# Value rows of a PEER layer consumed in pairs instead of fours

## The chip, the cores and the metric

One core of a Trainium2 chip runs the whole kernel. The metric is the device time of one execution in microseconds, the median of several runs. The trace numbers come from one profiled execution.

## What is computed

One decoder layer over 1024 positions of width 1024: a token mixer, cross-attention into 256 memory tokens, and a PEER layer, which is the part that the change touches. For each token and each of 8 heads, PEER picks 16 of 16384 single-neuron experts; `u` is the first table and `v` the second:

```python
def per_block(inp):
    xb, eb, gb = inp
    act = jnp.einsum('bthkd,btd->bthk', u[eb], xb).astype(jnp.float32)
    w = (gb * jax.nn.gelu(act, approximate=False)).astype(v.dtype)
    return jnp.einsum('bthk,bthkd->btd', w, v[eb])
```

So each token needs 128 rows of `u` (a dot product with each), and a weighted sum of the same 128 rows of `v`. A layer norm follows.

## The kernel before

The first two stages (the mixer, up to about 1000 us) are not touched. The third, `attend_and_retrieve`, handles tiles of 128 tokens, one token a partition. The first 6 tiles (GATHERED) fetch their expert rows by indirect DMA. The last 2 (DENSE) go through all 16384 experts by dense matrix products instead, in two halves of 64 blocks, woven into the same program.

**Slots.** All engines walk through the same 768 slots (6 tiles x 128 picks), each in its own program order, and meet only at semaphores. In slot g:

- POOL issues the gather of row g of the first table (line 1734, one row of 1024 floats a partition, 512 KB) into a ring of 8 places, then the gather of row g - 20 of the second table (line 1750) into another ring of 8 places. LAG is 20: the weight of a row is known only after its head's 16 dot products.
- DVE takes the dot product of row g with the token (line 2318), and pieces of the next tile's front work (top-16 search, norms).
- ACT spreads the weight of row g - 20 into a 128 x 32 matrix (`spread`, line 2078; `comb` holds four 32-row identities on top of each other), and after each head's 16 dots computes the gelu of 16 weights (line 2062).
- PE multiplies the rows of the second table into `acc` (`combine`, line 1783), runs a piece of the next tile's front (lines 1790 to 1852: transposes, attention scores and values, query and key products), and, from slot 381 on, about one tick a slot of the dense part: `choose` (line 1889, spreads the gates of the dense tokens over the experts of a half), then `dense_u` (line 1901) and `dense_v` (line 1918) for each block in turn.

**The combine.** The tokens of a tile are ordered so that a gathered row belongs to partitions by groups of 32. One matmul takes a spread (128 x 32) as weights and 512 columns of a row as the moving operand and writes the 32 partitions of `acc` that belong to place c = row mod 4. So a quad of rows (SIDE = 4) fills the four groups of 32 array columns side by side; with two halves of 512 columns it is 8 matmuls, each of which appears in the trace as two records. Everything is float32 and accumulates over the 32 quads of a tile; `start` is set on the first quad, `stop` on the last.

**Waits around it.** Each DMA adds 16 to a semaphore. Rows of the second table land on two semaphores (`v_landed`, V_QUADS = 2), quads in turn. PE runs a quad in the slot of its fourth row: it waits for the spreads (`diag_ready`), at the start of a tile for `acc` to have been read (`acc_copied`), and for all four rows; its last matmul adds 1 to `v_used`. POOL, before it gathers row g into a place, and ACT, before it overwrites a spread, wait until `v_used` shows that the quad of row g - 8 is done. With 8 places, the wait changes its value at each fourth row. The last 16 rows (FINAL) have places of their own and land on four semaphores, one for four rows. DVE's layer norm of a finished tile (`norm3_a`, line 2355) waits for `v_used` too and then frees `acc`.

The first half of the slots is filled with front work (each tile's front takes 45 slots). SP issues the dense tables' blocks (512 KB each of `u` and `v`) into rings of three.

## Time and profile before

| | us |
|---|---|
| median of 3 runs | 3616.82 |
| lowest and highest | 3611.86, 3619.35 |
| the profiled execution | 3633.32 (span 3631.3) |

| engine | busy us | share of the span |
|---|---|---|
| PE (matmuls) | 2950.5 | 81% |
| DVE | 2293.9 | 63% |
| POOL | 1848.1 | 51% |
| ACT | 1089.5 | 30% |

The mean granted clock of TensorE is 0.878 of its full rate. 1090.87 MB are moved, 805.40 of them by the indirect gathers. Busy time of PE is modelled from pipelined matmuls, so a share near 100% still leaves room in other kernels. The gathers begin at about 1060 us; from then on all engines have work, and which of them ends the waits has to be read stretch by stretch.

### The profile page before, as it was taken

Reading aid. Unit: us, or ns where it says so; the run is one execution under the profiler, and the core shown is the slowest. Engines: PE = TensorE matmul, PEld = TensorE weight load, DVE = VectorE, ACT = ScalarE, POOL = GpSimd, SP = SyncE. Lnnn points to the kernel's source line nnn. Section 1 sums busy time; section 2 is a strip of 40 time slices with the busy share of each in tenths; the row PEclk is TensorE's granted clock in tenths of the full one; section 3 lists DMA queues with packets and bytes.
Section 4 is the critical chain, followed back from the end, with each engine's and each line's share of the span. In section 5 each row is a group of like instructions: output and inputs, shape, how many; then the busy total and the mean of one; then the engine's idle time right before and its main releaser. Section 6 shows DMA issues by size and latency. Waiting matters only on the chain.

```text
span 3631.3 us, 40464 instructions
## 1 busy us (share of the span) xinstructions
PE 2950.5 (81%) x14096; PEld 1973.7 (54%) x14096; DVE 2293.9 (63%) x4963; ACT 1089.5 (30%) x2864; POOL 1848.1 (51%) x1672
## 2 busy tenths in 40 slices
PE   8999989999995666567756536799999967999994
PEld 6878876665562332323422203477776645777771
DVE  3440047887067677878878768776666667666665
ACT  3320035553123223324323212222222312332222
POOL 3332212221026666666665666666666656666655
PEclk9999999999998877778776766699999867999996
DMA  4322254332459998999999999999999988999998
GB/s 147 117 87 93 93 210 139 95 107 88 162 226 367 351 363 321 352 369 353 364 364 336 391 347 354 362 381 409 409 409 409 402 336 329 409 409 409 409 409 328
DMA packets 313149, 1090.87 MB, mean 300 GB/s; under 512 B 33265, under 2 KB 56433, under 8 KB 309633
## 3 DMA queue, kind: packets, MB, share of 16 engines
q0 software_dynamic: 221184, 805.40, 58.1%
q1 hardware_dynamic: 91776, 283.09, 20.5%
q8 instruction: 103, 1.69, 0.2%
q14 instruction: 86, 0.70, 0.1%
HBM read 1052.12 MB, written 36.24 MB: 300 GB/s over the span
## 4 chain that ended last, share of the span: by engine, by line
PE 23%; DVE 13%; DMA 11%; POOL 9%; issue 7%; another core or an unknown queue 7%; ACT 3%; POOLq 0%; DVEq 0%; ACTq 0%
DMA arena<-in_v_dram,idx_v 9%; PE small L1901 7%; PE wide L1918 6%; PE acc L1783 5%; POOL arena L1750 5%; DVE arena L2318 3%; POOL far_rows L1734 2%; POOL arena L1734 2%; DVE far_rows L2318 2%; PE small L1840 2%; DMA arena<-in_u_dram,idx 2%; DVE arena L2593 1%; ACT gelu_v L2062 1%; DVE arena L2591 1%
## 5 line engine op out<-in xcount | busy, mean ns | idle before, releaser
L1750 POOL DMA_INDIRECT arena<-in_v_dram,idx_v x752 | 801.9, 1066 | 686.5 <-PE acc L1783 357.4
L1783 PE MATMUL acc<-arena 128*32 128x512 f32 x3008 | 497.2, 778 | 423.9 <-DMA arena<-in_v_dram,idx_v 217.3
L1734 POOL DMA_INDIRECT arena<-in_u_dram,idx x480 | 498.3, 1038 | 344.3 <-DVE idx L2554 190.5
L1783 PEld LDWEIGHTS acc<-arena 128*32 128x32 f32 x3008 | 100.0, 129 | 693.4 <-issue 529.4
L1901 PE MATMUL small<-pwq 128*128 128x256 f32 x2048 | 467.0, 381 | 2.0 <-ACT memory_tables L2179 1.7
L1901 PEld LDWEIGHTS small<-pwq 128*128 128x128 f32 x2048 | 386.6, 190 | 84.1 <-issue 28.8
L2318 DVE CUSTOM_DVE_ANT_0 arena<-arena,wide 128x1024 f32<-128x1024 f32 x294 | 355.1, 1216 | 73.6 <-DMA arena<-in_u_dram,idx 44.1
L1734 POOL DMA_INDIRECT far_rows<-in_u_dram,idx x288 | 302.5, 1050 | 92.3 <-issue 81.7
L2318 DVE CUSTOM_DVE_ANT_0 arena<-arena,h 128x1024 f32<-128x1024 f32 x186 | 226.5, 1224 | 183.2 <-DMA arena<-in_u_dram,idx 180.2
L2318 DVE CUSTOM_DVE_ANT_0 far_rows<-far_rows,wide 128x1024 f32<-128x1024 f32 x176 | 212.8, 1216 | 60.8 <-DMA far_rows<-in_u_dram,idx 42.3
L2189 ACT ACTIVATE arena<-small 128x256 f32<-128x256 f32 x128 | 49.2, 385 | 656.0 <-PE small L1901 484.5
L2078 ACT ACTIVATE arena<-comb,w_v 128x32 f32<-128x32 f32 x768 | 198.9, 311 | 153.0 <-remote 60.5
L433 PE MATMUL group<-w_nat_high,x_parts 128*128 128x512 f32 x768 | 240.6, 395 | 3.8 <-ACT arena L572 3.8
L927 PE MATMUL mix_bank<-memory_tables,mixT 128*128 128x512 f32 x512 | 226.4, 598 | 3.6 <-ACT mixT L1178 3.6
L898 POOL TENSOR_TENSOR arena<-arena 128x512 f32<-128x512 f32 (+1 forms) x48 | 48.1, 1001 | 346.3 <-DVE arena L1288 344.5
L2062 ACT ACTIVATE gelu_v<-act_u 32x4 f32<-32x4 f32 x768 | 159.4, 208 | 206.1 <-DVE act_u L2318 144.7
L1889 PEld LDWEIGHTS small<-arena 128*128 128x128 f32 x1024 | 165.0, 253 | 90.4 <-issue 64.1
L433 PE MATMUL group<-x_parts,arena_rounded 128*128 128x512 f32 x864 | 202.0, 395 | 10.7 <-DVE x_parts L606 10.7
L1889 PE MATMUL small<-arena 128*128 128x64 f32 x1024 | 172.7, 341 | 43.6 <-DVE arena L2595 22.6
L2318 DVE CUSTOM_DVE_ANT_0 far_rows<-far_rows,h 128x1024 f32<-128x1024 f32 x112 | 136.5, 1223 | 97.2 <-DMA far_rows<-in_u_dram,idx 90.0
L433 PEld LDWEIGHTS group<-x_parts,arena_rounded 128*128 128x128 f32 x864 | 163.7, 190 | 49.4 <-issue 10.1
L1918 PE MATMUL wide<-arena_rounded 128*128 128x512 f32 x512 | 181.4, 436 | 0.0
(376 smaller groups left out, 4973.2 us busy)
## 6 DMA issues: line engine op xcount, KB each, us to landing
pwq<-in_uT_dram SPq DMA_DIRECT2D x128, 512.0 KB
pwq<-in_v_dram SPq DMA_DIRECT2D x128, 512.0 KB
arena<-in_w_nat_dram SPq DMA_DIRECT2D x6, 2048.0 KB, 8.6
nat_dram<-stage SPq DMA_DIRECT2D x48, 256.0 KB, 2.1
arena<-in_v_dram,idx_v POOLq DMA_INDIRECT x752
scanT_dram<-stage SPq DMA_DIRECT2D x22, 512.0 KB, 2.9
arena<-in_w_tr_dram SPq DMA_DIRECT2D x18, 512.0 KB, 3.7
arena<-csT_dram SPq DMA_DIRECT2D x8, 1024.0 KB, 4.8
```

Of the source, the lines that this page charges most:

```text
L433: last = pe.matmul(to, stationary(p, k), moving(q, k), start=(k == 0 and n == 0), stop=(k == KC - 1 and n == 2))
L927: last = pe.matmul(place["OUT"][:, c * 512:(c + 1) * 512], mixT[:, k, :], w_out[:, k, c * 512:(c + 1) * 512], start=(k == 0), stop=(k == 2 ...
L1734: pool.indirect_dma_start(out=u_row(g), out_offset=None, in_=peer_u, in_offset=bass.IndirectOffsetOnAxis(ap=idx[:, t % KEPT, n:n + 1], axis=0)
L1750: pool.indirect_dma_start(out=v_row(g), out_offset=None, in_=peer_v, in_offset=bass.IndirectOffsetOnAxis(ap=idx_v[:, t % KEPT, n:n + 1], a ...
L1783: last = pe.matmul(acc[c * QUAD:(c + 1) * QUAD, half * 512:(half + 1) * 512], spread_row(at), v_row(at)[:, half * 512:(half + 1) * 512], s ...
L1840: last = pe.matmul(small[:, q * P:(q + 1) * P], pwq[:, k, q * P:(q + 1) * P], hT[:, k, :], start=(k == 0), stop=(k == KC - 1))
L1889: last = pe.matmul(small[:, at:at + HALF_KEYS], hot2[:, q % 2, j, :], hot1[:, q % 2, j, :], start=True, stop=True)
L1901: last = pe.matmul(small[:, at:at + DT], uT_ring[:, i % STREAM, k, :], dense_hT[:, k, :], start=(k == 0), stop=(k == KC - 1))
L1918: last = pe.matmul(wide[:, at:at + 512], w, v[:, c * 512:(c + 1) * 512], start=(i % HALF_KEYS == 0 and n == 0), stop=(i % HALF_KEYS == HAL ...
L2062: last = act.activation(gelu_v[r * QUAD:(r + 1) * QUAD, h % 2, :].rearrange("p (b c) -> p b c", c=SIDE)[:, :, c], act_u[c * QUAD:(c + 1) * ...
L2078: act.activation(spread_row(g), comb[:, :], ACT.Copy, scale=w_v[:, h % 2, j:j + 1]).then_inc(diag_ready, 1)
L2318: dve.tensor_tensor_reduce(out=row, in0=row, in1=against, scale=1.0, scalar=0.0, op0=ALU.mult, op1=ALU.add, accum_out=act_u[:, (n // TOPK) ...
```

## The change

Rows of the second table are handled in pairs. They land on four semaphores in turn (V_PAIRS = 4) instead of two; PE waits for two rows, multiplies them (4 matmuls) and adds 1 to `v_used`, in each second slot instead of each fourth; POOL and ACT wait for the pair of row g - 8 instead of its quad; the norm waits for twice the count. The column group of a row is still its place mod 4, so a pair uses two of the four groups. The four semaphores of the last 16 rows stay as they are, but their rows are multiplied in pairs too. Ring size, bytes, gathers, spreads and matmuls stay the same in number.

```diff
--- before.py
+++ after.py
@@ -29,7 +29,8 @@
 U_RING = 8
 V_NEAR = 8
 V_RING = 8
-V_QUADS = 2
+V_PAIRS = 4
+PAIR = 2
 KEYS_ROW = 2
 QUAD = 32
 SIDE = 4
@@ -1492,7 +1493,7 @@
         VALUE_TABLE = 14
         FIRST_ALL = VALUE_TABLE + KC
         u_landed = [sem(f"u_landed{i}") for i in range(U_RING)]
-        v_landed = [sem(f"v_landed{i}") for i in range(V_QUADS)]
+        v_landed = [sem(f"v_landed{i}") for i in range(V_PAIRS)]
         final_landed = [sem(f"final_landed{i}") for i in range(FINAL // SIDE)]
         dot_done = sem("dot_done")
         gelu_done = sem("gelu_done")
@@ -1617,7 +1618,7 @@
 
         def v_signal(g):
 
-            return final_landed[final_place(g) // SIDE] if final_place(g) >= 0 else v_landed[g // SIDE % V_QUADS]
+            return final_landed[final_place(g) // SIDE] if final_place(g) >= 0 else v_landed[g // PAIR % V_PAIRS]
 
         def spread_row(g):
 
@@ -1746,7 +1747,7 @@
                     if final_place(g) == 0:
                         pool.wait_ge(vb_used, NKEYS)
                     elif V_RING <= g < SLOTS - FINAL:
-                        pool.wait_ge(v_used, (g - V_RING) // SIDE + 1)
+                        pool.wait_ge(v_used, (g - V_RING) // PAIR + 1)
                     pool.indirect_dma_start(out=v_row(g), out_offset=None, in_=peer_v,
                                             in_offset=bass.IndirectOffsetOnAxis(ap=idx_v[:, t % KEPT, n:n + 1], axis=0)
                                             ).then_inc(v_signal(g), 16)
@@ -1768,21 +1769,21 @@
                 def combine(t, s, n):
 
                     g = PICKS * t + n
-                    if n % SIDE < SIDE - 1:
+                    if n % PAIR < PAIR - 1:
                         return
                     pe.wait_ge(diag_ready, g + 1)
-                    if n == SIDE - 1 and t > 0:
+                    if n == PAIR - 1 and t > 0:
                         pe.wait_ge(acc_copied, t)
                     if final_place(g) >= 0:
                         pe.wait_ge(final_landed[final_place(g) // SIDE], 16 * SIDE)
                     else:
-                        pe.wait_ge(v_landed[g // SIDE % V_QUADS], 16 * SIDE * (g // SIDE // V_QUADS + 1))
+                        pe.wait_ge(v_landed[g // PAIR % V_PAIRS], 16 * PAIR * (g // PAIR // V_PAIRS + 1))
                     for half in range(2):
-                        for c in range(SIDE):
-                            at = g - SIDE + 1 + c
+                        for at in range(g - PAIR + 1, g + 1):
+                            c = at % SIDE
                             last = pe.matmul(acc[c * QUAD:(c + 1) * QUAD, half * 512:(half + 1) * 512],
                                              spread_row(at), v_row(at)[:, half * 512:(half + 1) * 512],
-                                             start=(n == SIDE - 1), stop=(n == PICKS - 1))
+                                             start=(n < SIDE), stop=(n >= PICKS - SIDE))
                     last.then_inc(v_used, 1)
 
                 def to_T(source):
@@ -2074,7 +2075,7 @@
                     if g == 0:
                         act.wait_ge(comb_ready, SIDE)
                     if V_RING <= g < SLOTS - FINAL:
-                        act.wait_ge(v_used, (g - V_RING) // SIDE + 1)
+                        act.wait_ge(v_used, (g - V_RING) // PAIR + 1)
                     act.activation(spread_row(g), comb[:, :], ACT.Copy,
                                    scale=w_v[:, h % 2, j:j + 1]).then_inc(diag_ready, 1)
 
@@ -2644,7 +2645,7 @@
                         elif n == 2 and t > 0:
                             weigh(t - 1, 1 - s, PHEADS - 1)
                         if n == LAG and t > 0:
-                            norm3_a(t, h2[:, 1 - s, :], acc[:, :], v_used, PICKS // SIDE * t)
+                            norm3_a(t, h2[:, 1 - s, :], acc[:, :], v_used, PICKS // PAIR * t)
                         if n == LAG + 4 and t > 0:
                             norm3_b(t, h2[:, 1 - s, :])
                         slot = PICKS * t + n
@@ -2665,7 +2666,7 @@
 
                 def last(t, s):
                     weigh(t - 1, 1 - s, PHEADS - 1)
-                    norm3_a(TILES, h2[:, 1 - s, :], acc[:, :], v_used, PICKS // SIDE * t)
+                    norm3_a(TILES, h2[:, 1 - s, :], acc[:, :], v_used, PICKS // PAIR * t)
                     norm3_b(TILES, h2[:, 1 - s, :])
 
                 tiles(body, last)
```

## Rows read from the trace of the kernel before

**Rows 1.** The page's slices: GB/s moved in each fortieth of the span.
```profile
GB/s 147 117 87 93 93 210 139 95 107 88 162 226 367 351 363 321 352 369 353 364 364 336 391 347 354 362 381 409 409 409 409 402 336 329 409 409 409 409 409 328
```
**Rows 2.** Stretches: length, then busy us (records) of PE, PEld, DVE, ACT, POOL; clock, DMA, GB/s.
```profile
1110.00:2060.00 950.00, 613.40 (x2952) 301.04 (x2951) 732.60 (x2191) 298.00 (x951) 603.18 (x618) 0.78 0.95 355
2060.00:2180.00 120.00, 39.57 (x202) 10.72 (x200) 82.41 (x299) 27.22 (x100) 74.99 (x80) 0.65 0.94 361
2180.00:2380.00 200.00, 136.89 (x750) 90.88 (x754) 167.59 (x249) 49.47 (x160) 131.38 (x135) 0.65 0.96 357
2380.00:2865.00 485.00, 467.08 (x2304) 350.78 (x2297) 305.86 (x524) 141.78 (x384) 302.96 (x252) 0.99 1.02 406
2865.00:3080.00 215.00, 148.33 (x833) 102.11 (x832) 156.17 (x238) 53.23 (x173) 133.54 (x134) 0.70 0.91 342
3080.00:3550.00 470.00, 454.02 (x2239) 342.33 (x2241) 295.53 (x508) 135.85 (x362) 290.10 (x242) 0.99 1.03 409
```
**Rows 3.** The same stretches, line 1783 alone: PE busy (records), PEld busy (records), clock, DMA.
```profile
1110.00:2060.00 950.00, 215.48 (x1248) 41.98 (x1248) 0.78 0.95 355
2060.00:2180.00 120.00, 35.06 (x160) 6.58 (x160) 0.65 0.94 361
2180.00:2380.00 200.00, 53.52 (x264) 10.12 (x268) 0.65 0.96 357
2380.00:2865.00 485.00, 64.43 (x508) 14.44 (x500) 0.99 1.02 406
2865.00:3080.00 215.00, 50.95 (x256) 9.53 (x256) 0.70 0.91 342
3080.00:3550.00 470.00, 60.37 (x492) 14.14 (x496) 0.99 1.03 409
sum 2521.00, PE 510.97 PEld 103.28; mean PE 73.00 PEld 14.75
```
**Rows 4.** Line 1783 from 1110 to 2060: ns of one record, min/median/max.
```profile
L1783 PE MATMUL acc<-arena x1248: 589/617/1063, 1112.2 to 2058.1; 128*32 128x512 f32 x179
```
**Rows 5.** Timeline of PE in a dense stretch: start, us, work, idle before it.
```profile
2574.68 1.92 PE L1783 MATMUL acc<-arena 128*32 128x512 f32 x16 [1.09 <-DMA arena<-in_v_dram,idx_v]
2576.53 3.72 PE L1901 MATMUL small<-pwq 128*128 128x256 f32 x16
```
**Rows 6.** Timeline of PE among front work of a gathering stretch.
```profile
1805.76 1.92 PE L1783 MATMUL acc<-arena 128*32 128x512 f32 x16
1807.61 7.13 PE L1808 MATMUL wide<-memory_tables,arena 128*128 128x512 f32 x16
...
1826.36 3.64 PE L1783 MATMUL acc<-arena 128*32 128x512 f32 x16 [9.15 <-DMA arena<-in_v_dram,idx_v]
```
**Rows 7.** Waits from 1110 to 2060: who <- releaser: us in total, times, longest us.
```profile
POOL arena L1750 <- remote: 100.8, 43, 4.1
PE acc L1783 <- DMA arena<-in_v_dram,idx_v: 78.9, 17, 10.5
POOL arena L1750 <- PE acc L1783: 72.5, 17, 12.0
PE acc L1783 <- ACT arena L2078: 63.5, 10, 16.1
```
**Rows 8.** Waits in the dense stretch from 2380 to 2865.
```profile
POOL arena L1750 <- PE acc L1783: 112.4, 29, 10.0
...
PE acc L1783 <- DMA arena<-in_v_dram,idx_v: 16.7, 14, 4.1
```
**Rows 9.** Timeline of POOL in the gathering stretch.
```profile
1807.75 0.94 POOL L1750 DMA_INDIRECT arena<-in_v_dram,idx_v  x1 [0.30 <-issue]
1809.00 0.94 POOL L1734 DMA_INDIRECT arena<-in_u_dram,idx  x1 [0.31 <-issue]
1812.43 0.94 POOL L1750 DMA_INDIRECT arena<-in_v_dram,idx_v  x1 [2.49 <-remote]
```
**Rows 10.** The end of PE's work in its timeline.
```profile
3615.32 6.16 PE L1783 MATMUL acc<-memory_tables,arena 128*32 128x512 f32 x40 [1.08 <-issue]
```

## The prediction

> **What bounds the kernel now.** The table of stretches is read first [rows 1, 2]. From 1110 to 3631 us the rows of the two tables are gathered, and this part has two regimes. In the two stretches with the dense products of the last tokens (2380 to 2865 and 3080 to 3550), the DMA engines move 406 and 409 GB/s, the flat maximum of the slices [rows 1], and at the same time PE is busy for 467.1 of 485 and 454.0 of 470 us. Two resources are full at once. In the others neither is: from 1110 to 2060 PE is busy for 613.4 of 950 us at a mean granted clock of 0.78, DVE for 732.6, and 355 GB/s are moved. The second reading is PE's line 1783 alone [rows 3], the third what four rows cost PE [rows 4 to 6], the fourth who waits in each regime [rows 7 to 9].
>
> **How many combines.** A quad leaves 16 matmul records. The dense stretches hold 508 + 492 = 1000 records, 62.5 quads in 955 us, one each 15.28 us. The stretch from 1110 to 2060 holds 1248, 78 quads, one each 12.18 us, a slot (one row of each table) each 3.05 us. The stretches 2180 to 2380 and 2865 to 3080, where PE picks the gates of the dense tokens, hold some 32.
>
> **What a pair costs on PE.** This is the term that decides. A quad's 16 records take 1.92 us though one record takes 592 or 617 ns [rows 4, 5]: 16 one after another would be 9.5 us or more. A full-width record of the same 512 columns comes each 7.13 / 16 = 0.446 us [rows 6]. So 1.92 us is four rounds of about 0.43 us plus one tail of about 0.19, four records side by side in each round, one for each group of 32 columns. A group of columns has four records to run (two halves, two records each) whatever its neighbours do. A pair has 8 records, two in each of the same four rounds: 1.92 us as a quad, and twice in four slots. Rivals of this price: 0.96 us, if a combine's time goes by its records and not by its rounds (then the change adds nothing), and 8 x 0.446 = 3.6 us, if nothing ran side by side. I take 1.85 us, the time from a quad's first record to the start of the next work (2574.68 to 2576.53), since the rounds fit the quad's rows with nothing left over. Where the clock is low a quad takes 3.64 us [rows 6]; the mean from 1110 to 2060 is 215.48 / 78 = 2.76 us.
>
> A combine also switches PE between column groups and the full array. The Trainium skill, TensorEngine Tiling (Array Packing), Key Properties, says that a change of the tiling mode drains the engine. No row shows a drain by itself. The 1.85 us holds what the way out of a quad costs, and the sum would be the same with a drain named.
>
> **Part by part.** The four spreads on ACT, the gathers on POOL and the bytes stay the same in number: no cost. The waits on PE grow from one set in four slots to two; they are sequencer work, counted at nothing where the condition holds.
>
> *Dense stretches.* PE's work is 467.08 + 454.02 = 921.1 us. It gets 62.5 more combines x 1.85 = 115.6, so 1036.7 us, more than the 955 us there are. If all its idle time (33.9 us, mostly the wait for landed rows, 16.7 us in the first stretch [rows 8]) vanishes, the stretches grow by 81.7 us; if it all stays, by 115.6. The wait should mostly go, as rows come in more often than PE can take them: **+88**. POOL's stall here (112.4 us on PE's line 1783 in the first stretch [rows 8]) costs nothing today, because the queue behind it is full at 406 GB/s; freeing places earlier buys nothing.
>
> *Gathering stretch 1110 to 2060.* This is where the change can win. POOL issues a gather each 1.24 us [rows 9], so eight (four of each table) take 9.95 us, against 12.18. The difference is its stalls: 100.8 us put down to "remote" and 72.5 to PE [rows 7], 173.3 in all. All of them stand before the first row of a quad, as in [rows 9] (2.49 us): that row needs the release of the quad two back, whose last row was issued five slots earlier. In pairs, the row needs a pair whose last row was issued seven slots earlier: two slots, about 5 us, more room. Most stalls are shorter than that, and would go. But three floors stand below. POOL: 950 - 173.3 = 777 us. DMA: 355 x 950 / 409 = 825 us. PE: 613.4 + 215.5 (the combines again, at their mean of today) = 829 us. PE is the highest, and it can't run full: it waits today for landings (78.9 us) and for ACT's spreads (63.5 us) [rows 7]. Kept whole, these 142 us bring 971 us, 21 more than today; gone, 829, 121 less. As PE falls behind the gathers, landings are there when it comes, but the spreads' chain (DVE's dots, ACT's gelu, DVE's product) is not shortened, and it now holds PE at the second row and not at the fourth. I keep some 76 us, about half: 829 + 76 = 905, **-45**, from +21 to -121.
>
> *Stretches 2180 to 2380 and 2865 to 3080.* PE 136.9 + 148.3 = 285.2, plus 53.5 + 51.0 = 104.5, is 389.7 of 415 us, 94%. Little to win, little to lose: **+5**, from -25 to +40.
>
> *2060 to 2180.* PE has only combines: 39.6 + 35.1 = 75 of 120 us, hidden. Eight gathers take 12 us as before against 9.95 at POOL's own pace, most of it in one long stall: **-5**, from 0 to -18 (10 quads at 2 us, less what DMA holds back).
>
> *Start of a tile.* The first combine of a tile waits until DVE has taken acc over, now two slots earlier. At five tile borders this costs nothing if DVE is in step, up to 2 x 3.05 us each (30 us) if it lags as far; no row shows PE waiting for it: 0, the other end goes into the range.
>
> *The end.* The last 16 rows are still waited for in fours but multiplied in pairs. Behind the last wait 40 records run in 6.16 us with nothing beside them [rows 10]; their rounds nearly double: **+5**, from +2 to +6.
>
> Sum: 88 - 45 + 5 - 5 + 5 = **+48 us**. The profiled execution took 3633.32 us (span 3631.3), 16.5 above the median of the runs; the same difference is carried over: 3633.3 + 48 = 3681 profiled, 3616.8 + 48 = **3665** as median.
>
> **Rivals.**
>
> *The room wins (faster).* The gathering stretch falls to its floor. What would bring it there is the clock: rows with a busier PE show a higher granted clock (0.99 at 96% busy, 0.78 at 65%, 0.65 at 33%) [rows 2]. If twice the combines lift the clock to the higher of its two levels, 2.4 GHz, a quad's 2.76 us becomes 1.92, PE's floor falls to about (613.4 - 215.5) x 0.78 + 2 x 78 x 1.92 = 610 us, and DMA's 825 decides: -125; with -25 and -18 in the other two and +82 and +5 that is -81: 3536. Against it: 0.65 and 0.70 at 68% busy between 2180 and 3080, so the link is loose, and DVE at 733 of 825 us would be 89% full in an order of its own. It decides the sign as soon as the stretch from 1110 to 2060 gives back more than the dense stretches take, that is from some 85 us on. The Trainium skill, TensorE: Matmul & The Clock Gate, in the part on the clock gate, says that the throttled state is the default and activity releases it; by that rule this case is the likelier one, and the rows agree in direction only.
>
> *The pair is cheap (faster).* At 0.96 us a pair, dense stretches +0 and the gathering stretch -121: about 3490.
>
> *It comes out even.* PE keeps a third of its waits in the gathering stretch and the pick stretches gain 10: within 7 us of 3617.
>
> *PE is late everywhere (slower still).* None of its waits shrinks: +116, +21, +40, 0, +6: 3800; with half of that beyond my sum 3735. It decides where the wait for spreads moves two slots up at each head.
>
> *The change does nothing at the ring.* If the stalls called "remote" are no matter of places but of the release itself coming late (PE's quad at 1805.76 is over at 1807.68 [rows 6], POOL goes on at 1812.43 [rows 9]), each pair could bring such a stall, and the gathering stretch gains nothing: +93, 3710. This is inside the slower side.
>
> **How the numbers follow.** A measurement of this kernel can tell about 0.2% (7 us) from no change. Forecast, PE as bound with part of the stalls won back: 0.48. The release rival: 0.12. PE late everywhere: 0.08. Even: 0.06. The room wins: 0.20. Cheap pair: 0.06. So slower 0.68, same 0.06, faster 0.26. The likeliest case's own range is 3625 to 3710; to hold eight in ten the range reaches up to half of the late case and down to near the rival in which the room wins: 3555 to 3745.
>
> **What would show it.** In the profile after: 8 records of line 1783 in 1.9 us in the dense stretches (1.0 would be the cheap pair), so that its busy time goes from 511 us towards 950; dense stretches over 1020 us long, PE at 97% or more there, and GB/s under 380 with POOL's stalls on PE still there; from 1110 on, the part of POOL's idle time before line 1750 halved, with PE over 85% busy. Wrong if the dense stretches keep their 955 us, or if the gathering stretch ends more than 90 us earlier.

## The result, and the profile after

| | before, us | after, us |
|---|---|---|
| median | 3614.34 (4 runs) | 3692.52 (4 runs) |
| lowest and highest | 3608.30, 3619.35 | 3691.01, 3703.22 |
| profiled execution | 3633.32 | 3691.36 |

The ratio is 1.0221, with a 95% interval of 1.0188 to 1.0253: the change makes the kernel slower by 78 us, where 48 were forecast (3665). The median of before is over one run more than the 3616.82 that the forecast started from. The two profiled executions differ by 58 us, because that of before lay 19 us above its own median of 3614.34 and that of after 1 us below its own.

For where the 58 us are, each trace is cut at the same instructions: the first gather of the second table, the first transpose of the dense tokens, the first record of the dense products in each half (line 1901 of before), the first record of `choose` of the second half, and the last record of the dense products (line 1918). "Picking" stands for the two gate-picking stretches. All tables of stretches below are made in this way, in us, from these starts:

| | gathering | picking 1 | dense 1 | picking 2 | dense 2 | tail |
|---|---|---|---|---|---|---|
| before | 1035.1 | 264.0 | 492.2 | 193.0 | 481.0 | 77.7 |
| after | 1040.3 | 256.0 | 532.0 | 178.1 | 524.0 | 71.8 |
| difference | +5.2 | -8.0 | +39.8 | -14.9 | +43.0 | -5.9 |

The differences add up to 59, because after the first gather came 1 us earlier. The dense stretches took 82.8 us more, against the forecast's 88. The gathering stretch, which was to give 45 back, gave nothing, and the gate-picking stretches and the tail gave 29 where next to nothing was expected.

After, in stretches that answer to [rows 2] (length; busy us and records of PE, PEld, DVE, ACT, POOL; clock, DMA share, GB/s):
```profile
1105.00:2058.00 953.00, 703.23 (x2976) 305.61 (x2972) 730.35 (x2199) 300.43 (x958) 611.50 (x625) 0.87 0.96 358
...
2383.00:2915.00 532.00, 527.44 (x2296) 357.67 (x2296) 302.67 (x532) 145.63 (x394) 287.23 (x252) 1.00 0.99 378
2915.00:3093.00 178.00, 146.99 (x754) 83.95 (x752) 138.25 (x211) 43.93 (x154) 114.62 (x120) 0.81 0.95 350
3093.00:3617.00 524.00, 523.46 (x2285) 356.72 (x2286) 296.54 (x522) 141.01 (x382) 285.11 (x250) 1.00 0.99 377
```
In both dense stretches PE is busy for 99% of the time or more (527.4 of 532, 523.5 of 524) and DMA has fallen from 406 and 409 GB/s to 378 and 377: of the two resources that were full, PE alone now sets the time, although the DMA share still reads 0.99. After, the combine's line alone (PE, PEld, clock, DMA share, GB/s), which answers to [rows 3]:
```profile
1105.00:2058.00 953.00, 327.44 (x1248) 62.44 (x1244) 0.87 0.96 358
...
2383.00:2915.00 532.00, 121.51 (x504) 23.93 (x504) 1.00 0.99 378
```
As many records as before take 121.5 us in place of 64.4. After, PE's timeline in a dense stretch (start, us, work), to be held against [rows 5]:
```profile
2506.13 1.91 PE L1784 MATMUL acc<-arena 128*32 128x512 f32 x8
2507.97 3.72 PE L1902 MATMUL small<-pwq 128*128 128x256 f32 x16
...
2514.37 1.91 PE L1784 MATMUL acc<-arena 128*32 128x512 f32 x8
```
Eight records of a pair take as long as a quad's sixteen, and pairs come each 8.24 us, so four slots take 16.48 us in these rows, against a mean of 15.28 before. After, who waits, in the gathering stretch (who <- releaser: us, times, longest), against [rows 7]:
```profile
PE acc L1784 <- ACT arena L2079: 88.4, 27, 12.7
PE acc L1784 <- issue: 83.3, 21, 15.9
...
POOL arena L1751 <- remote: 69.6, 30, 4.3
POOL arena L1751 <- PE acc L1784: 67.9, 37, 8.6
```
and in the first dense stretch, against [rows 8]:
```profile
ACT arena L2190 <- PE small L1902: 284.5, 50, 6.7
POOL arena L1751 <- PE acc L1784: 183.9, 62, 7.0
```
PE's 78.9 us of waiting for landed rows don't appear in the gathering stretch after, those for spreads grew from 63.5 to 88.4, and POOL's two stalls shrank only from 173.3 to 137.5. The wait for rows isn't simply gone: "issue", idle time for which the profile shows no releaser, was at the same line before
```profile
PE acc L1783 <- issue: 52.6, 19, 16.0
```
and is 83.3 us now. In all PE sat idle before its combines for 195.0 us before and 171.7 after.

### The profile page after: what moved, and what is told of

Read it like the earlier page. It is cut to its first block, busy times and chain, and to the rows that moved or that the text cites. A ratio compares the mean times of both kernels' runs of the same rounds, so it can differ in the third digit from the quotient of the medians.

```text
span 3689.4 us, 40656 instructions
## 1 busy us (share of the span) xinstructions
PE 3197.0 (87%) x14096; PEld 1973.7 (53%) x14096; DVE 2272.0 (62%) x4963; ACT 1088.7 (30%) x2864; POOL 1815.2 (49%) x1672
## 4 chain that ended last, share of the span: by engine, by line
PE 39%; DVE 16%; issue 7%; another core or an unknown queue 6%; ACT 3%; POOL 2%; DMA 1%; POOLq 0%; DVEq 0%; ACTq 0%
PE small L1902 12%; PE acc L1784 10%; PE wide L1919 10%; DVE arena L2319 4%; DVE far_rows L2319 3%; PE small L1890 2%; PE wide L1809 1%; PE small L1841 1%; ACT gelu_v L2063 1%; POOL arena L1751 1%; PE wide L1824 1%; DVE arena L2594 1%; DVE idx_v L2552 1%; DVE gates_v L2552 1%
## 5 line engine op out<-in xcount | busy, mean ns | idle before, releaser
L1751 POOL DMA_INDIRECT arena<-in_v_dram,idx_v x752 | 764.4, 1017 | 742.3 <-PE acc L1784 460.3
L1784 PE MATMUL acc<-arena 128*32 128x512 f32 x3008 | 798.1, 675 | 306.0 <-ACT arena L2079 169.4
L1735 POOL DMA_INDIRECT arena<-in_u_dram,idx x480 | 496.4, 1034 | 368.8 <-DVE idx L2555 190.7
L1784 PEld LDWEIGHTS acc<-arena 128*32 128x32 f32 x3008 | 153.7, 117 | 743.5 <-issue 530.2
L2319 DVE CUSTOM_DVE_ANT_0 arena<-arena,wide 128x1024 f32<-128x1024 f32 x294 | 353.7, 1212 | 34.7 <-DMA arena<-in_u_dram,idx 14.3
L2603 DVE TENSOR_TENSOR memory_tables<-memory_tables,arena 128x256 f32<-128x256 f32 x128 | 55.2, 432 | 432.6 <-ACT arena L2190 229.6
L434 PE MATMUL group<-x_parts,arena_rounded 128*128 128x512 f32 x864 | 201.9, 395 | 10.9 <-DVE x_parts L607 10.9
L1890 PEld LDWEIGHTS small<-arena 128*128 128x128 f32 x1024 | 136.8, 212 | 101.4 <-issue 84.0
L1890 PE MATMUL small<-arena 128*128 128x64 f32 x1024 | 147.2, 299 | 33.2 <-issue 28.1
## 6 DMA issues: line engine op xcount, KB each, us to landing
nat_dram<-stage SPq DMA_DIRECT2D x48, 256.0 KB, 2.2
```

The costliest lines, as they stand in the source:

```text
L434: last = pe.matmul(to, stationary(p, k), moving(q, k), start=(k == 0 and n == 0), stop=(k == KC - 1 and n == 2))
L1735: pool.indirect_dma_start(out=u_row(g), out_offset=None, in_=peer_u, in_offset=bass.IndirectOffsetOnAxis(ap=idx[:, t % KEPT, n:n + 1], axis=0)
L1751: pool.indirect_dma_start(out=v_row(g), out_offset=None, in_=peer_v, in_offset=bass.IndirectOffsetOnAxis(ap=idx_v[:, t % KEPT, n:n + 1], a ...
L1784: last = pe.matmul(acc[c * QUAD:(c + 1) * QUAD, half * 512:(half + 1) * 512], spread_row(at), v_row(at)[:, half * 512:(half + 1) * 512], s ...
L1890: last = pe.matmul(small[:, at:at + HALF_KEYS], hot2[:, q % 2, j, :], hot1[:, q % 2, j, :], start=True, stop=True)
L2319: dve.tensor_tensor_reduce(out=row, in0=row, in1=against, scale=1.0, scalar=0.0, op0=ALU.mult, op1=ALU.add, accum_out=act_u[:, (n // TOPK) ...
```

## The experiments

They ran in three sets, each with runs of the kernel before among them. The kernel before had a median of 3448.77 us in the first set, 3631.82 in the second and 3447.88 in the third, so only kernels of one set are compared in time. "Theory" and the letters stand for what each expectation says.

### First set: the price of a pair

The kernel before and the change again, to have both traces in this set:

> The kernel before, profiled a second time. The result is 78 us slower by the medians, but the two profiled executions differ by 58 us only; the first profile of before lay 19 us above its median. Theory: this is one slow profiled execution, and a second profile of before has its span near 3612, the missing 20 us in the gathering stretches (up to the first dense product at 2387 us), where semaphores decide, not in the dense stretches, which a full DMA queue fixes at 492 and 481 us. Rival: profiling itself costs before 16 to 19 us and the second profile repeats 3630.

> The changed kernel again, on one chip with the others. Expected 3690 to 3700 us and 1.019 to 1.025 of before; dense stretches of 532 and 524 us as in its first profile.

Before: 3447.58 us in its one run. After: 3529.82 (3526.40 to 3530.46), a ratio of 1.0233 (1.0217 to 1.0249). The ratio and the dense stretches (532.1 and 524.0 us, table below) are as expected. The times are not, and neither 3612 nor its rival 3630 for the trace of before can be judged, since the gathering and gate-picking stretches are faster here.

`fours_by_two` keeps fours, but orders the quad's matmuls as two pairs one after the other:
```diff
-                    for half in range(2):
-                        for c in range(SIDE):
-                            at = g - SIDE + 1 + c
+                    for first in (0, 2):
+                        for half in range(2):
+                            for c in (first, first + 1):
+                                at = g - SIDE + 1 + c
...
```


> Waits, ring and releases in fours as before; only the order of a quad's 8 matmuls is changed: rows 0 and 1 with both halves, then rows 2 and 3, so that two column groups work side by side and not four. It has PE's price without the granularity of two. Theory (the price is rounds on PE): the 8 matmuls take 7 to 8 rounds of 0.43 us, 3.2 to 3.8 us for 1.9, the two dense stretches grow by 70 to 100 us together, the gathering stretch by 20 to 80, and the whole is at or above the changed kernel: 3690 to 3780. Rival (records count, not rounds; the slower time comes from waiting in pairs): 1.9 us a quad and 3615.

3449.34 us (3444.89 to 3459.10), ratio 1.0006 (0.9997 to 1.0016): no difference. The theory, 3.2 to 3.8 us a quad, is refuted. The rival's numbers came, though not for its reason, since eight records of the change take as long as sixteen. `pairs_crossed` is the change with the second half of each row moved to the two column groups that the pair leaves idle. The accumulator's second half then lies in other partitions, and the norm reads it from there:
```diff
-                            c = at % SIDE
+                            c = (at + 2 * half) % SIDE
...
-                    dve.scalar_tensor_tensor(y3, y3, ALPHA, total, ALU.mult, ALU.add).then_inc(acc_copied, 1)
...
+                        dve.scalar_tensor_tensor(y3[:, 0:HALF_D], y3[:, 0:HALF_D], ALPHA, total[:, 0:HALF_D], ALU.mult, ALU.add)
+                        for to, source in ((slice(0, 64), slice(64, 128)), (slice(64, 128), slice(0, 64))):
+                            last = dve.scalar_tensor_tensor(y3[to, HALF_D:D], y3[to, HALF_D:D], ALPHA,
+                                                            total[source, HALF_D:D], ALU.mult, ALU.add)
...
```


> Waits, ring and releases in pairs as in the changed kernel, but the second half of a row's columns goes to the column group two places on, so that a pair's 4 matmuls fill all four groups: two rounds a pair, four rounds in four slots as before. The norm puts the halves right with two more vector operations at each of the 6 tiles (about 0.6 us each). It has the granularity of two without PE's price. Theory: a pair takes 1.0 to 1.1 us, the dense stretches come back to 960 to 980 us, and what pairs bring by themselves shows in the gathering stretch: its stalls on line 1750 fall from some 160 us to under 100, for 3560 to 3600 in all, faster than before. Rival 1 (granularity brings nothing, the gathering stretch is held by the chain of dots, gelu and spreads): 3610 to 3625. Rival 2 (each combine has a fixed cost that twice as many pay): 3640 or more.

3466.68 us (3465.32 to 3471.95), ratio 1.0058 (1.0044 to 1.0072): slower than before, not faster as its theory had it. A quad in `fours_by_two`, and a pair in `pairs_crossed`, in the dense stretch (PE's timeline of each):
```profile
2408.70 1.94 PE L1784 MATMUL acc<-arena 128*32 128x512 f32 x16 [1.15 <-DMA arena<-in_v_dram,idx_v]
```
```profile
2403.59 1.06 PE L1784 MATMUL acc<-arena 128*32 128x512 f32 x8
```

| first set | gathering | picking 1 | dense 1 | picking 2 | dense 2 | tail |
|---|---|---|---|---|---|---|
| before | 925.9 | 228.1 | 490.5 | 159.0 | 480.9 | 76.8 |
| after | 935.5 | 223.7 | 532.1 | 152.4 | 524.0 | 72.2 |
| `fours_by_two` | 926.2 | 228.4 | 490.2 | 159.0 | 480.7 | 76.9 |
| `pairs_crossed` | 926.0 | 239.0 | 484.9 | 173.3 | 475.5 | 78.1 |

The order in which a quad's matmuls are issued doesn't matter (1.94 us): within a batch the four groups of columns still run side by side. What costs is that a pair offers work to only two of the four groups. With all four in use the same 8 records take 1.06 us, and the 84.7 us that the dense stretches of the change cost here not only vanish but turn into a gain of 11.0. The gathering stretch gained nothing from the pairs (926.0 against 925.9). The Trainium skill, TensorEngine Tiling (Array Packing), Key Properties, states that different tiles can load weights and multiply in parallel; 1.06 and 1.91 us for the same eight records show what it means when only half of them have work.

But `pairs_crossed` loses 10.9 and 14.3 us in the gate-picking stretches. Its stretches (columns as above):
```profile
2014.00:2253.00 239.00, 198.98 (x871) 124.56 (x871) 207.94 (x373) 63.18 (x207) 166.15 (x172) 0.51 1.00 392
...
2738.00:2911.00 173.00, 171.05 (x753) 117.41 (x752) 147.03 (x223) 44.88 (x155) 119.87 (x123) 0.50 1.01 394
```
and those of the kernel before in this set:
```profile
2010.00:2238.00 228.00, 154.68 (x874) 96.92 (x870) 206.76 (x375) 63.10 (x206) 166.08 (x173) 0.66 1.02 400
2729.00:2888.00 159.00, 113.19 (x753) 76.50 (x753) 144.58 (x220) 45.14 (x155) 117.70 (x122) 0.81 1.02 407
```
PE, with half the time per pair, is granted 0.51 and 0.50. In the second of these stretches it is busy for 171 of 173 us: at the lower of its two levels it has become the bound there. In the first it is busy for 199 of 239. This gave a theory for the second and third sets.

### Second set: price without the finer waits, and the clock

`fours_in_two_parts` is the kernel before, with places 0 and 1 of a quad multiplied where the quad was and places 2 and 3 after the slot's other work:
```diff
+                    multiply(g, n, (0, 1))
+
+                def multiply(g, n, places):
                     for half in range(2):
-                        for c in range(SIDE):
+                        for c in places:
...
-                    last.then_inc(v_used, 1)
+                    return last
+
+                def combine_rest(t, s, n):
+                    if n % SIDE == SIDE - 1:
+                        multiply(PICKS * t + n, n, (2, 3)).then_inc(v_used, 1)
...
                             dense(tick)
+                        if n >= LAG or t > 0:
+                            combine_rest(*lagged(t, s, n))
...
```


> The kernel before, its waits, its four-row releases and its two landing semaphores unchanged; only PE's work of a quad is cut in two: places 0 and 1 are multiplied where the quad was, places 2 and 3 after the same slot's front or dense work. So PE pays the price of pairs (two batches that each use two of the four column groups) while nothing is waited for or given back in pairs. Theory A (the price of a pair on PE is the whole loss of the dense stretches): each batch of 8 records takes 1.9 us, the dense stretches are 80 to 86 us longer than before's 971 (490 and 481), the rest within 5 us, a ratio of 1.020 to 1.026, as the change itself has. Theory B (the loss comes from waiting or releasing in pairs): dense stretches within 10 us of before, a ratio of 0.998 to 1.004.

3752.50 us (3749.28 to 3758.76), ratio 1.0342 (1.0309 to 1.0375). Its timeline and its first dense stretch:
```profile
2459.54 1.91 PE L1786 MATMUL acc<-arena 128*32 128x512 f32 x8
...
2464.35 1.91 PE L1786 MATMUL acc<-arena 128*32 128x512 f32 x8
...
2476.04 1.91 PE L1786 MATMUL acc<-arena 128*32 128x512 f32 x8
```
```profile
2422.00:2954.00 532.00, 527.51 (x2304) 357.63 (x2304) 307.91 (x533) 145.63 (x394) 303.51 (x255) 1.00 0.99 379
```
The dense stretches are those of the change to the tenth (532.3 and 524.1 against 532.0 and 524.0), four slots in 16.50 us in these rows, though it waits and releases in fours. So in these stretches the price of the two batches is the whole loss, as theory A had it. The ratio is above A's range all the same: outside of them this kernel takes 1600.8 us, against 1558.0 to 1585.3 of the three others of its set (below), while the change was 24 us shorter there than before in its own set. Its release comes only after the second batch, later than that of before, so how much of the excess is the batch and how much the lateness isn't told apart.

The next two kernels put matmuls with zero weights, which add nothing to the sum, ahead of a batch, outside of the dense stretches. `fours_zeros` does it to the kernel before and `crossed_zeros` to `pairs_crossed` (the lines shown are those of `crossed_zeros`):
```diff
+        def outside(g):
+
+            slot = g + LAG
+            dense = any(tick_slot(h * HALF_TICKS + GROUP_TICKS) <= slot < (tick_slot(HALF_TICKS), DENSE_END)[h] for h in range(2))
+            return slot >= DENSE_AT and not dense
...
+                    if outside(g) and n > SIDE:
+                        pe.wait_ge(zeros_ready, 1)
+                        for half in range(2):
+                            for at in range(g - PAIR + 1, g + 1):
+                                c = (at + 2 * half) % SIDE
+                                pe.matmul(acc[c * QUAD:(c + 1) * QUAD, half * 512:(half + 1) * 512],
+                                          zeros[:, :], v_row(at)[:, half * 512:(half + 1) * 512], start=False, stop=False)
```


> The kernel before, with each quad's 8 matmuls preceded by 8 more whose weights are zero (they add nothing to the sum), outside the dense stretches alone: in the two stretches in which PE picks the gates, the one just before the first, and the tail. It asks what the granted clock does when PE has some 2 us more work in four slots there, while waits and releases stay in fours. Theory A (the changed kernel's shorter gate-picking stretches come from a higher granted clock that its busier PE gets): clock there from 0.66 and 0.81 up to 0.80 and 0.93 or so, the two stretches 4 to 8 us shorter in sum than before's 387, a ratio of 0.996 to 0.999. Theory B (they come from waiting and releasing in pairs): the clock may rise but the stretches don't shorten, or grow by up to 15 us with the added work: 1.000 to 1.005.

3648.97 us (3632.28 to 3652.76), ratio 1.0039 (1.0020 to 1.0059).

> The crossed pairs (the two halves of a pair go to different column groups, so all four run), with 4 more zero-weight matmuls ahead of each pair's 4, outside the dense stretches alone. The crossed pairs were 11 us shorter than before in the dense stretches and 25 us longer in the two gate-picking stretches, where the granted clock was 0.51 and 0.50. Theory A (those 25 us are the clock's, which fell because PE had less to do): the clock there is 0.8 or more, the stretches return to the plain pairs' 376 in sum against 412, dense stays at 960, and the kernel is 15 to 25 us below before, 0.993 to 0.996. Theory B (they come from another cause, such as the norm's read of the crossed accumulator): clock up or not, the stretches stay over 400, 1.004 to 1.008.

3616.79 us (3598.58 to 3626.38), ratio 0.9961 (0.9941 to 0.9982). `mixed` takes pairs only where `outside` holds for the quad (`in_pairs`), and fours elsewhere, with the release counted in pairs throughout:
```diff
+        def used(g):
+
+            return g // PAIR + 1 if in_pairs(g) else 2 * (g // SIDE + 1)
...
-                        pool.wait_ge(v_used, (g - V_RING) // SIDE + 1)
+                        pool.wait_ge(v_used, used(g - V_RING))
...
-                    last.then_inc(v_used, 1)
+                    last.then_inc(v_used, size // PAIR)
```


> Fours in the gathering and in the two dense stretches, plain pairs (waited for, multiplied and given back) only in the two gate-picking stretches and the tail, with four landing semaphores throughout. Theory A (a pair costs in the dense stretches alone, where PE and DMA are both full, and gains 11 us in the gate-picking stretches and 5 in the tail): dense 971, gate-picking 376 in sum against 387, tail 72 against 77, a ratio of 0.995 to 0.998. Theory B (the gain in those stretches only answers the state that the pairs elsewhere leave, such as the rows already waiting): within 0.1% of before or above.

3620.87 us (3614.14 to 3636.16), ratio 0.9984 (0.9965 to 1.0002).

| second set | gathering | picking 1 | dense 1 | picking 2 | dense 2 | tail |
|---|---|---|---|---|---|---|
| `fours_in_two_parts` | 1055.7 | 273.7 | 532.3 | 190.7 | 524.1 | 80.7 |
| `fours_zeros` | 1042.6 | 269.6 | 492.4 | 181.7 | 479.2 | 91.4 |
| `crossed_zeros` | 1019.7 | 275.6 | 484.5 | 187.8 | 473.8 | 84.7 |
| `mixed` | 1032.9 | 269.0 | 487.9 | 178.2 | 481.3 | 77.9 |

This set has no trace of the kernel before. `fours_zeros` and `mixed` do the same work in fours up to the first gate-picking stretch, and they differ by 9.7 us there: a stretch of one execution can't be read closer than some 10 us here. Their second gate-picking stretch, `fours_zeros` first:
```profile
2897.00:3079.00 182.00, 151.88 (x1000) 88.46 (x992) 143.09 (x219) 44.73 (x154) 118.52 (x121) 0.79 0.96 353
```
```profile
2878.00:3056.00 178.00, 141.50 (x752) 80.38 (x752) 142.35 (x218) 44.49 (x155) 116.27 (x121) 0.83 0.98 373
```
The gate-picking stretches of `fours_zeros` are no shorter than those of `mixed`, the clock is no higher, and the tail is 13.5 us longer. Theory A's ratio and its clock for the second stretch (0.93) didn't come, and the whole kernel lost 17 us, most of it in the tail. Without a trace of before in this set it isn't known whether its gate-picking stretches are shorter than before's, so where the clock comes from is left open by it. `crossed_zeros` has the better ratio and the 958 us of dense stretches of A, but its gate-picking stretches (463.4 us in sum) are longer than those of `mixed` (447.2); A's 376 came from a set with faster gathers and can't be held against them. `mixed` lies within its interval of no change. Its dense stretches (969.2) are as A had them, its tail is not: 77.9 us with pairs, where A had 72 and before has 76.3 to 77.7 in all its traces. So pairs in the tail alone don't shorten it, which speaks for B there; for the rest its theories are neither shown nor refuted.

### Third set: the clock on its own

The kernel before, the change, the crossed pairs again, and the crossed pairs with zeros in the gate-picking stretches alone:
```diff
-            return slot >= DENSE_AT and not dense
+            return DENSE_AT <= slot < DENSE_END and not dense
```


> The kernel before, once more, for a trace of it on the same chip as the next three. No theories differ. On the first chip its stretches from the first row of the second table on were 1035, 264, 492, 193, 481 and 78 us (gathering, gate-picking, dense, gate-picking, dense, tail).

> The changed kernel, once more. Theory A (the price of a pair on PE is paid in the dense stretches wherever it runs, the rest depends on the chip): dense stretches together 80 to 86 us over those of the trace of before on this chip, 20 to 30 less in the other four together if gathering runs at 355 GB/s, 0 to 10 less if it runs at 400; ratio 1.020 to 1.026. Theory B (the loss depends on the chip): anything outside that.

> The crossed pairs without zero-weight matmuls. On one chip they were 11 us shorter in the dense stretches and 25 longer in the gate-picking ones, with a granted clock of 0.51 and 0.50. Theory A (the clock falls because PE's work per pair is halved): the clock in the gate-picking stretches is below that of before here (0.50 to 0.60), these stretches are 10 to 30 us longer in sum than with zeros, ratio 1.002 to 1.008. Theory B (the crossed kernel without zeros is as fast as with them, and the zeros only cost): clock 0.65 or more, ratio 0.993 to 0.998. If rows gather at 355 GB/s here, the gathering stretch tells what the pair's price on PE took from it: crossed pairs 10 to 25 us shorter there than the changed kernel (PE's share) or within 5 us (DMA's).

> The crossed pairs with 4 zero-weight matmuls a pair in the gate-picking stretches alone, no longer in the tail, where four-row records with zeros had made it 14 us longer (91 against 78). Theory A (the zeros are worth their price where PE has other work to bring under the higher clock, and cost where only combines are left): the tail 5 to 9 us shorter than the 85 us with zeros, the rest as with them, ratio 0.991 to 0.996. Theory B (the tail's length follows the clock, and without zeros it grows by as much): ratio 0.996 to 0.999.

| third set | median, us | ratio | gathering | picking 1 | dense 1 | picking 2 | dense 2 | tail |
|---|---|---|---|---|---|---|---|---|
| before | 3447.88 | | 923.2 | 228.2 | 490.2 | 156.8 | 483.3 | 76.3 |
| after | 3524.06 | 1.0224 (1.0204 to 1.0245) | 935.3 | 222.5 | 532.0 | 150.0 | 524.0 | 72.2 |
| `crossed_third` | 3465.03 | 1.0050 (1.0035 to 1.0065) | 925.8 | 239.0 | 484.9 | 173.1 | 476.3 | 77.0 |
| `crossed_zeros_choose` | 3443.30 | 0.9990 (0.9981 to 0.9999) | 926.3 | 222.6 | 490.9 | 157.9 | 480.3 | 78.7 |

The trace of before is its one run of 3446.53 us. The change does what theory A of its expectation says: +82.5 us in the dense stretches, 4.5 less in the other four together. For `crossed_third` the clock and the ratio are theory A's; its gate-picking stretches are 31.6 us longer than with zeros, where A had 10 to 30. `crossed_third`, PE's timeline in the second gate-picking stretch, and below it the same of `crossed_zeros_choose`:
```profile
2802.49 1.94 PE L1784 MATMUL acc<-arena 128*32 128x512 f32 x8
2804.35 3.68 PE L1890 MATMUL small<-arena 128*128 128x64 f32 x16
2807.96 1.94 PE L1784 MATMUL acc<-arena 128*32 128x512 f32 x8
```
```profile
2812.25 1.06 PE L1793 MATMUL acc<-arena,zeros 128*32 128x512 f32 x8
2813.13 1.04 PE L1798 MATMUL acc<-arena 128*32 128x512 f32 x8
```
Their rows of the two gate-picking stretches, `crossed_third` first:
```profile
2014.00:2253.00 239.00, 198.94 (x871) 124.23 (x871) 207.80 (x373) 63.15 (x207) 167.25 (x172) 0.51 1.00 392
...
2738.00:2911.00 173.00, 171.30 (x753) 117.70 (x753) 147.06 (x223) 45.02 (x155) 119.95 (x124) 0.50 1.01 395
```
```profile
2013.00:2236.00 223.00, 159.48 (x1107) 86.12 (x1104) 206.52 (x370) 63.29 (x207) 165.41 (x170) 0.80 1.02 405
...
2727.00:2885.00 158.00, 139.02 (x994) 80.76 (x995) 144.19 (x219) 45.31 (x156) 116.89 (x122) 0.87 1.02 405
```
With 29% more records (2101 against 1624), PE is busy for 72 us less: at 0.50 a pair and its share of `choose` follow each other without a gap, 5.47 us in two slots; with zeros the clock is 0.80 and 0.87 and the two stretches are 31.6 us shorter. That is shown, by adding work alone: the crossed kernel's 25 to 27 us in these stretches were the clock's. The Trainium skill, TensorE: Matmul & The Clock Gate, in its Part 1, says that the gate is set by "how busy the PE has been recently"; here more work brought more clock, though the share of busy time in the records was the higher one (171 of 173 us) at the lower level.

Yet the dense stretches, 12 us under before in `crossed_third`, give 10 of these back. The stretches of picking and dense 1 together take 718.4 us before, 723.9 crossed and 713.5 with zeros; those of the second half 640.1, 649.4 and 638.2. With zeros the DMA share is 1.02 or 1.03 and the rate 404 to 409 GB/s in every stretch up to the tail. The reading is that the bytes set the time there, so a cheaper combine has nothing to win: length times GB/s gives 491 x 409 = 200.8 MB in dense 1 with zeros and 485 x 403 = 195.5 in `crossed_third`, whose slow gate-picking stretch had moved most of the difference beforehand. The tail is 78.7 us against 77.0 without zeros anywhere. The 84.7 us it was to be measured against belong to another set, but the tail of before hardly differs between the sets, so this speaks for theory A's tail without settling it. The total (0.9990) is outside theory A's range and at the edge of B's. Of all kernels run, the crossed pairs with zeros are the only ones whose interval lies below the kernel before: 0.9961 in the second set, with zeros in the tail too, and 0.9990 here. No run shows a use of the pair that is worth more than that.

## Why the prediction was right or wrong

**The price of a pair: right.** Four rounds whatever the number of groups, 1.92 us at the full clock; it measured 1.91. Its two rivals (0.96 and 3.6 us) fell in the trace after, and `pairs_crossed` and `fours_by_two` show why it is so. 1.06 us for crossed pairs also bears out the rounds of about 0.43 us and one tail of about 0.19: two rounds and the tail are 1.05.

**The dense stretches: right.** +88 forecast, +82.8, +84.7 and +82.5 in the three traces of after beside one of before, close to the floor of 81.7 at which PE has no idle time left. `fours_in_two_parts`, with the same dense stretches and the waits of before, shows that waiting in pairs has no part in it.

**The gathering stretch: wrong.** -45 was forecast, +5.2, +9.6 and +12.1 measured. The step that failed is the one that makes PE the bound there, 829 us of work plus 76 us of kept waits. Both parts were mis-sized. The clock rose to 0.87 and a pair cost 327.44 / 156 = 2.10 us in place of a quad's 2.76, so PE had work for 703 of 953 us, not for 829. And its idle time before was 950 - 613 = 337 us, of which only the 142 of two waits were counted: by the same sum the kernel before would have taken 613 + 142 = 755 us there. After, 250 us of idle time are left, and PE's work doesn't set the length.

The second step that failed is the room: "two slots, about 5 us, more room", by which most of POOL's stalls would go. The records of line 1750 and of the combines can be matched by their order. Before, 45 of the 78 gathers of a quad's first row start more than 0.6 us after both the modelled end of the quad that they need and the end of POOL's instruction before; after, 42 of 156 at the first row of a pair; in the third set 6 of 83 and 4 of 168. So for most stalls called "remote" (100.8 us before, 69.6 after) the place was free already, and more room could not help. They are in the slower gatherings alone. What they are was not found.

DMA's floor, "355 x 950 / 409 = 825", is not what failed in the sum, as 905 lies above it. In the first and third sets the gathering stretch of before is full (before of the third set):
```profile
1100.00:2010.00 910.00, 604.18 (x3073) 291.48 (x3074) 786.49 (x2387) 319.46 (x1032) 646.15 (x669) 0.82 1.02 403
```
and there no handling of places can win. For the traces of the prediction (355 GB/s at a share of 0.95 [rows 2], 406 at 1.02 in the dense stretch) the share would give an estimate of 950 x 0.95 / 1.02 = 885 us. But the dense stretches of after, where PE is the bound, read 0.99, so a share near 1 doesn't show that the bytes decide. The traces' packets tell more. In the first dense stretch, 166 of 48739 packets of 4 KB took over 200 ns before, and 1785 of 48962 after. In the gathering stretch 3806 of 82249 did before and 3856 of 83012 after, but 659 of 88450 in the third set. By this the slower gathering is like a stretch that the bytes don't bound. What bounds it, neither PE's work nor plainly the bytes, stays open.

**Gate-picking stretches and tail: wrong in size and, for the tail, in sign.** +5 (and a part of the -5) was forecast and -22.9 measured, -11.0 and -12.5 in the other sets; the tail -5.9 instead of +5. The cause is not shown. The first of these stretches lies ahead of both dense ones. In the third set, before and then after, it is
```profile
2010.00:2238.00 228.00, 155.43 (x871) 95.79 (x871) 207.49 (x375) 63.40 (x207) 165.09 (x171) 0.66 1.02 400
```
```profile
2023.00:2246.00 223.00, 169.31 (x873) 85.71 (x872) 206.00 (x368) 63.33 (x207) 166.98 (x172) 0.88 1.03 409
```
The same 91.2 MB (length times GB/s) moved at a higher rate, with a higher granted clock. For the second one and the tail the rows suggest a coupling: a dense stretch that gets longer leaves DMA room, in which rows and blocks land ahead. Of the third set, before and then after, from the first dense stretch to the end:
```profile
2238.00:2728.00 490.00, 468.20 (x2304) 351.93 (x2304) 308.68 (x524) 145.67 (x392) 295.75 (x254) 0.99 1.03 408
2728.00:2885.00 157.00, 131.75 (x757) 91.91 (x754) 143.80 (x220) 44.90 (x155) 117.17 (x120) 0.69 1.02 406
2885.00:3368.00 483.00, 466.88 (x2287) 351.84 (x2288) 305.85 (x521) 140.61 (x381) 293.13 (x250) 0.99 1.03 408
3368.00:3444.00 76.00, 27.12 (x147) 5.85 (x145) 37.43 (x58) 16.39 (x61) 44.78 (x42) 0.72 0.84 326
```
```profile
2246.00:2778.00 532.00, 527.81 (x2298) 357.61 (x2298) 304.17 (x534) 145.31 (x392) 285.30 (x251) 1.00 0.99 382
2778.00:2928.00 150.00, 123.13 (x753) 74.65 (x753) 138.86 (x211) 44.99 (x155) 113.88 (x119) 0.97 1.01 396
2928.00:3452.00 524.00, 524.00 (x2288) 356.80 (x2287) 297.47 (x524) 141.08 (x385) 286.57 (x252) 1.00 0.99 382
3452.00:3523.00 71.00, 34.79 (x145) 8.77 (x144) 35.95 (x55) 15.57 (x57) 41.20 (x38) 0.70 0.82 310
```
Here length times GB/s gives 199.9 and 197.1 MB in the dense stretches before, 203.2 and 200.2 after; 63.7 and 24.8 MB in the second gate-picking stretch and the tail before, 59.4 and 22.0 after. Some 3 MB more moved in each dense stretch and as much less behind it. 4.3 MB less at 406 GB/s are 10.6 us, which covers the 6.8 us that the stretch is shorter, at its somewhat lower rate. In the trace of the prediction the row of before is
```profile
2880.00:3073.00 193.00, 130.51 (x753) 89.77 (x754) 143.41 (x220) 45.20 (x156) 119.45 (x122) 0.68 0.90 337
```
and the same reckoning gives 65.0 MB against 62.3 (178 us at 350 GB/s), so about half of the 15 us there. But by the packets its dense stretches moved only 200.9 and 197.3 MB after against 200.1 and 196.0 before. And `fours_in_two_parts`, with dense stretches as long, moved 532 x 379 = 201.6 and 524 x 374 = 196.0 MB in them and has 190.7 and 80.7 us behind them. So a longer dense stretch alone is not enough; if bytes go ahead, it takes the waits or releases in pairs as well. No run tried that by itself. At the very end, after:
```profile
3672.34 1.91 PE L1784 MATMUL acc<-memory_tables,arena 128*32 128x512 f32 x13 [1.87 <-DMA memory_tables<-in_v_dram,idx_v]
3674.44 1.05 PE L1784 MATMUL acc<-memory_tables,arena 128*32 128x512 f32 x3 [0.19 <-issue]
3677.41 2.20 PE L1784 MATMUL acc<-memory_tables,arena 128*32 128x512 f32 x16 [1.91 <-DMA memory_tables<-in_v_dram,idx_v]
```
Only 16 records are left behind the last landing, in 2.20 us, where 40 in 6.16 us were counted as the work to be doubled [rows 10]. The other pairs were done by then.

**The start of a tile** was put at nothing, with 30 us as the other end. No row of after lists PE waiting for the norm at the combine's line in the gathering stretch, so nothing speaks against it.

**From the profiled execution to the median: 19 us.** The difference of 16.5 us between before's execution and its median was carried over to after, which had none. Against the medians the sum (48) is 30 short; 10 of these are the terms, 20 this step. That the terms are only 10 off is luck: the gathering stretch missed by 50 us one way, and the dense and gate-picking stretches and the tail by 39 the other.

**The rivals.** The room wins: the clock did rise, as it says (0.78 to 0.87), but the stretch was bound elsewhere, so the step from clock to time failed. Cheap pair: refuted at 1.91 us. The release rival had the gathering stretch gain nothing and gave 3710, and both its number for that stretch and its total are the nearest of all. It is half right: the "remote" stalls were no matter of places. But each pair did not bring one (30 in 156 pairs, where 78 quads had 43), and what they are stays open. PE late everywhere: at the combine's line the wait for spreads grew by 25 us and "issue" by 31, but the wait for rows fell by more.

## What to carry to other kernels

Before a batch is made smaller, ask whether it fills the array by its width: a batch of matmuls that run side by side costs its longest group, so half a batch costs the whole, twice. Before an engine's work and waits are called a floor, see that they add up to the stretch as it is today: here 613 + 142 us left 195 of 950 out. A DMA share of 0.95 or 0.99 doesn't show that the bytes set the time. Where two resources are full at once, freeing one of them buys almost nothing (0.9990 with a combine of half the price and the clock kept up), and loading one alone costs in full (1.022).

## What the runs showed of the hardware

- **Order within a batch.** Sixteen records in the order of two pairs take 1.94 us, in the order of one quad 1.92.
- **Half a batch costs the whole.** Eight records on two of the four column groups take 1.91 us, eight on all four 1.06, sixteen on all four 1.92.
- **The clock can fall because work got cheaper.** Halving the combine's time (third set) brought the granted clock from 0.66 and 0.69 to 0.51 and 0.50 in the gate-picking stretches, the lower of the two levels (1.2 GHz) nearly throughout, and cost 27 us; useless matmuls brought it back.
- **The same kernel at 3448 and at 3632 us.** In the three traces of the kernel before the dense stretches agree within 2.4 us (490 to 492, 481 to 483), the gathering stretch does not: 923 and 926 against 1035 us, at 403 GB/s with a share of 1.02 against 355 to 358 with 0.95. From 1110 us on, the trace of the prediction has, in 950 us, 337.58 MB in 92561 packets; the third set's has in 910 us:
```profile
DMA packets 99551, 363.02 MB, mean 403 GB/s; under 512 B 11043, under 2 KB 11043, under 8 KB 99493
```
Half of the 4 KB packets take 159 ns or less in the slower one and 161 in the faster; the means are 174 and 164, because 3806 of 82249 against 659 of 88450 take over 200. What makes the gathering slower was not found. It need not be the chip: the second set (3632 us) and the third (3448) ran on a chip of the same number. The ratio of the change was the same wherever it was measured (1.0221, 1.0233, 1.0224).
